# The gate as four wide products, and moved halves and stores, in a one-core diffusion layer

## The reference

```python
def adaln(cond, w_ada, b_ada):
    mod = jax.nn.silu(cond) @ w_ada + b_ada
    shift, scale, gate = jnp.split(mod[:, None, :], 3, axis=-1)
...
        h_l = rmsnorm(x_l, norm_g[l]) * (1.0 + sc) + sh
        u_l = h_l @ w_in[l]
...
        out_l = mixer(u_l, keys_all, lp, rope, True)
...
        x_l = x_l + gt * (out_l @ w_out[l])
    return rmsnorm(x_l, final_norm_g)
```

## Time and profile before

| | us |
|---|---|
| median of 3 runs | 985.48 |
| lowest and highest | 983.87, 987.82 |
| the profiled execution, its own time | 985.1 |
| its span, first to last instruction | 983.3 |
| PE busy | 951.1 (97%) |
| DVE busy | 619.1 (63%) |
| ACT busy | 398.9 (41%) |
| POOL busy | 95.6 (10%) |

### The profile page before, as it was taken

How to read it: one execution, slowest core, us unless ns; L and a number is a source line. 1 busy time by engine, 2 the same in 40 slices (tenths; PEclk the granted TensorE clock), 3 DMA queues, 4 the chain that set the end, 5 groups by cost and what they waited for, 6 DMA issues and landing times.

```text
span 983.3 us, 12611 instructions
## 1 busy us (share of the span) xinstructions
PE 951.1 (97%) x5074; PEld 788.2 (80%) x5074; DVE 619.1 (63%) x821; ACT 398.9 (41%) x626; POOL 95.6 (10%) x77
## 2 busy tenths in 40 slices
PE   5999999989999999999999999999999999999996
PEld 3777787778888889888888888888888888888885
DVE  2776989777756676746785563767777765513154
ACT  3555665544234433322323432645445452212224
POOL 1222200300002200000003360000000000202020
PEclk8999999999999999999999999999999999999999
DMA  9999922222232221258784233101002117222224
GB/s 366 426 423 395 339 87 84 86 65 65 86 95 86 72 80 43 86 171 292 257 300 149 86 87 127 43 12 43 12 1 86 44 57 286 86 86 86 95 77 171
DMA packets 28838, 136.17 MB, mean 138 GB/s; under 512 B 3595, under 2 KB 4043, under 8 KB 21740
## 3 DMA queue, kind: packets, MB, share of 16 engines
q1 hardware_dynamic: 28060, 134.71, 38.2%
q10 hardware_dynamic: 720, 0.66, 0.2%
HBM read 131.16 MB, written 4.19 MB: 138 GB/s over the span
## 4 chain that ended last, share of the span: by engine, by line
PE 77%; DVE 11%; DMA 5%; ACT 4%; issue 2%; SPq 0%; ACTq 0%; DVEq 0%
PE pp L1717 28%; PE pp L2023 18%; PE pp L1747 17%; PE pp L1664 4%; PE pp L1641 2%; DMA w_raw<-in_wb_dram 2%; PE pp L1986 2%; DMA wa_raw<-in_wa_dram 2%; DMA ada_raw<-in_w_ada_dram 1%; PE pp L1668 1%; DVE w_lo L1139 1%; DVE gate_acc L1150 1%; DVE pt_lo L1409 1%; ACT w_hi L616 1%; PE pp L1978 1%
## 5 line engine op out<-in xcount | busy, mean ns | idle before, releaser
L1717 PE MATMUL pp<-h_hi,w_hi 128*128 128x512 f32 x544 | 215.9, 397 | 2.1 <-DVE w_lo L1139 1.2
L1717 PE MATMUL pp<-h_lo,w_hi 128*128 128x512 f32 x544 | 213.1, 392 | 0.0
L1717 PE MATMUL pp<-h_hi,w_lo 128*128 128x512 f32 x544 | 212.8, 391 | 0.0
L1139 DVE TENSOR_TENSOR w_lo<-w_raw,w_hi 128x1024 fp32r<-128x1024 f32 x68 | 87.2, 1282 | 100.7 <-ACT w_hi L616 100.4
L616 ACT ACTIVATE w_hi<-w_raw 128x1024 fp32r<-128x1024 f32 x68 | 72.0, 1058 | 176.7 <-PE pp L1717 129.4
L1717 PEld LDWEIGHTS pp<-h_hi,w_hi 128*128 128x128 f32 x544 | 102.9, 189 | 27.1 <-DVE w_lo L1139 4.2
L1717 PEld LDWEIGHTS pp<-h_hi,w_lo 128*128 128x128 f32 x544 | 102.8, 189 | 21.9
L1717 PEld LDWEIGHTS pp<-h_lo,w_hi 128*128 128x128 f32 x544 | 103.0, 189 | 21.4 <-issue 0.8
L2023 PE MATMUL pp<-wo_hi,m_hi 128*128 128x512 f32 x256 | 100.6, 393 | 0.0
L2023 PE MATMUL pp<-wo_hi,m_lo 128*128 128x512 f32 x256 | 99.6, 389 | 0.0
L2023 PE MATMUL pp<-wo_lo,m_hi 128*128 128x512 f32 x256 | 99.6, 389 | 0.0
(11 more groups left out here) (309 smaller groups left out, 1874.8 us busy)
## 6 DMA issues: line engine op xcount, KB each, us to landing
w_raw<-in_wb_dram SPq DMA_DIRECT2D x68, 512.0 KB, 3.6
ada_raw<-in_w_ada_dram SPq DMA_DIRECT2D x15, 2048.0 KB, 12.2
w_gate_raw<-in_w_gate_dram SPq DMA_DIRECT2D x16, 1024.0 KB, 4.9
wo_raw<-in_w_out_dram SPq DMA_DIRECT2D x16, 1024.0 KB, 4.7
wa_raw<-in_wa_dram SPq DMA_DIRECT2D x16, 320.0 KB, 7.0
UG<-in_xT_dram SPq DMA_DIRECT2D x8, 512.0 KB, 8.4
y<-in_x_dram SPq DMA_DIRECT2D x4, 1024.0 KB, 9.2
wh_raw<-in_w_heads_dram SPq DMA_DIRECT2D x4, 768.0 KB, 4.7
```

What stands on the lines that cost most here:

```text
L1139: eng.tensor_tensor(lane(wb_lo, n % KW), lane(wb_raw, n % KW), lane(wb_hi, n % 2), ALU.subtract).then_inc(wb_lo_done, 1)
L1717: mm = eng.matmul(ps[i][:], w, x, start=(kk == 0 and m == 0), stop=(kk == KT - 1 and m == 2))
```

## The change

- **Gate sums**: `gate_sums` now makes 4 products, with the 128x128 tile of ones as the weights and 512 columns of `gate_acc` as the moving side. Each gives the sums in all 128 rows alike, in banks 2, 3, 6 and 7. At n = 65 DVE's `gate_rows_done` adds them to `gate_rows`, where SP has put the bias row 128 times by a DMA of its own; SP issues it at its n = 65, behind the load of chunk 65, and first waits for `pool_done`. `gate_rows` lies in tiles 25 to 28 now. PE waits for `gate_out` before the first head. `gcol`, its bias columns in `par`, and the diagonals with their products and copy are gone.
- **Places of `w_out`**: the second and third place of `wo_raw` move; their first loads wait for the last values (`v_mm`) and the last scores (`s_mm`, 32).
- **Root**: on ACT at n = 9 the three `context_shift` come behind root, `turned` and `biased`.
- **Key halves**: on DVE at i = 6 `keys(2 * p + 2, 1)` comes ahead of `gate` and `rope_low`.
- **Last tile**: of the last token tile ACT scales block 0 alone and stores it, then stores block 3; POOL scales block 1; SP stores blocks 2 and 1.

```diff
-        wo_places = (FREE, 25, FREE + 5)
+        wo_places = (FREE, FREE + 5, FREE + 10)
...
+                if slot == 63:
+                    eng.wait_ge(pool_done, 4)
+                    eng.dma_start(gate_rows_[:], t["b_gate"].to_broadcast([P, D])).then_inc(gate_in[0], 16)
...
             load_out(0)
-            eng.wait_ge(pool_done, 4)
+            eng.wait_ge(v_mm, 12)
             load_out(1)
-            eng.wait_ge(v_mm, 12)
+            eng.wait_ge(s_mm, 32)
             load_out(2)
...
+            eng.wait_ge(gained, 12)
+            eng.wait_ge(row_scale, 4)
+            yy = y_out[:, 3 * D + L:3 * D + 2 * L]
+            eng.tensor_scalar(yy, yy, rs[:, 11:12], None, ALU.mult).then_inc(gained, 1)
...
-                for q in range(2):
+                for q in range(1 if tok == 3 else 2):
...
-                    if tok == 3:
-                        eng.wait_ge(fin_act, 7 + q)
-                        eng.dma_start(out[3 * P:4 * P, q * L:(q + 1) * L], yy).then_inc(stored, 16)
+            eng.wait_ge(fin_act, 7)
+            eng.dma_start(out[3 * P:4 * P, 0:L], y_out[:, 3 * D:3 * D + L]).then_inc(stored, 16)
+            eng.wait_ge(fin_done, 8)
+            eng.dma_start(out[3 * P:4 * P, 1536:D], y_out[:, 3 * D + 1536:4 * D]).then_inc(stored, 16)
...
-            def gate_columns():
+            def gate_rows_done():
                 eng.wait_ge(comb_mm, KT + 1)
-                eng.tensor_tensor(gcol[:], ps[7][:, 0:16], par[:, P_BG:P_BG + 16], ALU.add)
+                eng.wait_ge(gate_in[0], 16 * 8 + 16)
+                for i, b in enumerate((2, 6)):
+                    x = gate_rows_[:, i * 1024:(i + 1) * 1024].rearrange("p (a b) -> p a b", a=2)
+                    ins = eng.tensor_tensor(x, psum[:, b:b + 2, :], x, ALU.add)
+                ins.then_inc(gate_out, 1)
...
-            for i in range(16):
-                if i >= 4:
-                    eng.wait_ge(gate_mm, i - 3)
-                eng.tensor_scalar(out_tmp[:, (i % 4) * P:(i % 4 + 1) * P], ident[:], gcol[:, i:i + 1], None, ALU.mult).then_inc(diag_done, 1)
-            eng.wait_ge(gate_mm, 16)
-            eng.tensor_copy(gate_rows_[:].rearrange("p (a b) -> p a b", a=4), psum[:, 4:8, :]).then_inc(gate_out, 1)
...
-                for c in range(16):
-                    mm = eng.matmul(ps[7][:, c:c + 1], gate_acc[:, c * P:(c + 1) * P], ones[:, 0:1], start=True, stop=True)
+                for c, b in enumerate((2, 3, 6, 7)):
+                    mm = eng.matmul(ps[b][:], ones[:], gate_acc[:, c * L:(c + 1) * L], start=True, stop=True)
...
-            for i in range(16):
-                eng.wait_ge(diag_done, i + 1)
-                eng.matmul(psum[:, 4 + i // 4, (i % 4) * P:(i % 4 + 1) * P], ones[:], out_tmp[:, (i % 4) * P:(i % 4 + 1) * P],
-                           start=True, stop=True).then_inc(gate_mm, 1)
```

More of the change, by code:

```diff
@@ L31 @@
 HF = L // 2
-P_BSH, P_BSC, P_BG, P_NG = 0, 16, 32, 48
-P_CW, P_CB, P_HB, P_QG, P_KG, P_PS = 64, 100, 112, 120, 124, 126
-N_PAR = 130
+P_BSH, P_BSC, P_NG = 0, 16, 32
+P_CW, P_CB, P_HB, P_QG, P_KG, P_PS = 48, 84, 96, 104, 108, 110
+N_PAR = 114
 T_POOL, T_Q = 13, 17
@@ L142, in backbone @@
         wo_high_ = [at("wo_hi0", 19, 2048, F32R), at("wo_hi1", FREE + 16, 2048, F32R)]
-        gate_rows_, gain, y_out = at("gate_rows", FREE + 10, D), at("gain", TAB + 10, D), at("y", FREE + 21, 4 * D)
+        gate_rows_, gain, y_out = at("gate_rows", 25, D), at("gain", TAB + 10, D), at("y", FREE + 21, 4 * D)
         out_tmp, ss, rs = at("out_tmp", TAB + 14, L), at("row_sums", TAB + 15, 16), at("row_scale", TAB + 15.25, 12)
@@ L287, in backbone @@
         wo_in = [sem(f"wo_in{s}") for s in range(3)]
-        mix_hi, mix_lo, diag_done, gate_mm, gate_out = sem("mix_hi"), sem("mix_lo"), sem("diag_done"), sem("gate_rows_mm"), sem("gate_out")
+        mix_hi, mix_lo, gate_out = sem("mix_hi"), sem("mix_lo"), sem("gate_out")
         wo_hi, wo_lo, wo_mm, mm_done = sem("wo_hi_done"), sem("wo_lo_done"), sem("wo_mm"), sem("wo_bank_mm")
@@ L444, in _ @@
             for i in range(4):
[L445 to L448, removed]
+                eng.wait_ge(fin_done, 2 * i + (1 if i == 3 else 2))
+                a, b = 1024, 1536 if i == 3 else D
+                eng.dma_start(out[i * P:(i + 1) * P, a:b], y_out[:, i * D + a:i * D + b]).then_inc(stored, 16)
                 if i < 3:
                     eng.wait_ge(fin_act, 2 * i + 2)
-                    eng.dma_start(out[i * P:(i + 1) * P, 0:1024], y_out[:, i * D:i * D + 1024]).then_inc(stored, 16)
+                    a, b = 0, 1024
+                else:
+                    eng.wait_ge(gained, 13)
+                    a, b = L, 2 * L
+                eng.dma_start(out[i * P:(i + 1) * P, a:b], y_out[:, i * D + a:i * D + b]).then_inc(stored, 16)
             eng.wait_ge(stored, 160)
@@ L895, in _ @@
                         context(i)
-                if n == 9:
-                    for i in range(3):
-                        context_shift(i)
                 if n == 12:
@@ L947, in _ @@
                             product_high(m)
+                if n == 9:
+                    for i in range(3):
+                        context_shift(i)
                 if n % 4 == 3 and n not in (TF[0] + 3, TF[1] + 3):
@@ L1556, in _ @@
                 if i == 6:
+                    if p < 3:
+                        keys(2 * p + 2, 1)
                     gate(2 * p)
@@ L1590, in _ @@
                     rope_low(2 * p + 2)
-                    keys(2 * p + 2, 1)
                 if i == 7:
@@ L1905, in _ @@
             eng.wait_ge(kr_cut, 4)
+            eng.wait_ge(gate_out, 1)
             def queries(h):
@@ L2117, in alloc @@
             return ctx.enter_context(nc.sbuf_tensor(name, [P, cols], F32))
-        mem = {n: alloc(n, c) for n, c in (("par", N_PAR), ("gcol", 16), ("ident", P), ("ones", P), ("eps", 1))}
+        mem = {n: alloc(n, c) for n, c in (("par", N_PAR), ("ident", P), ("ones", P), ("eps", 1))}
         base = (nc.sbuf_base + 31) // 32 * 32
@@ L2201, in layout @@
         "w_heads": np.ascontiguousarray(w_heads),
-        "x": np.ascontiguousarray(f["x"][0]), "gain": f["final_norm_g"].reshape(1, D),
+        "x": np.ascontiguousarray(f["x"][0]), "gain": f["final_norm_g"].reshape(1, D), "b_gate": b_ada[2 * D:].reshape(1, D),
         "w_out": np.ascontiguousarray(f["w_out"][0].reshape(4, 4, P, 4, L).transpose(3, 0, 2, 1, 4)).reshape(16, P, 4 * L),
```

11 lines of the change are left out of this document (4 added, 7 removed).

## The result

The changed kernel takes **973.73 us** (median of 4 runs, 973.39 to 974.10); the kernel before, run on the same chip beside it, takes 985.10 (983.87 to 987.82). The ratio is 0.9886, with a 95% interval of 0.9874 to 0.9899. The forecast was 973.5. The profiled execution of the changed kernel took 973.39, with a span of 971.6 us against 983.3.

The account below looks back on a forecast made before the run. TensorE, busy 97% of 983.3 us, was taken as the bound. Gains 4.64 + 0.0 + 1.78 + 3.57 + 1.89 + 0 = 11.88 gave a forecast median of 973.5 us (971.5 to 975.5; wider range 971.5 to 978.5).

Parts of the forecast that it names:

- Root: Step 9 on ACT: earlier root removes 3.05 us of PE's wait and 1.59 of slow-clock products; gain 4.64 us.
- Rival A: Slow clock behind the root gap and gate sums does not come back; 1.59 + 1.78 lost, 976.9 us; chance 0.10.
- Gate sums: Four wide products cost the same as 16 one-column ones, but the clock stays up behind them; gain 1.78 us, bounds 0 to 1.9.
- Gate rows: Output stage: 16 diagonal products between two chunks disappear from PE, DVE's replacement additions are hidden; gain 3.57 us.
- The bias row: Its 1 MB DMA on SP ahead of chunk 66's load takes some 4.9 us and delays nothing PE needs; cost 0.
- can push it by about 1.3: Delay in us that the bias row's load could cause to chunk 66's load behind it, to 588.4.
- Rival C: Slower: bias row lands late and DVE stands still in step 65; 31 us after issue would give 990.8; chance 0.03.
- Keys: Heads, sixth step of a pair: k_lo moved in front removes three PE waits of 0.63; gain 1.89 us, bounds 0 to 2.1.
- Rival B: Waits are replaced: PE, earlier, meets the next wait (pt_lo, or ACT's moved activations); 975.4 to 978.4 us; chance 0.12.
- Places and waits of `w_out`: Later loads are wanted only after the last head; 0 taken, up to 4.9 us for a late load.
- Last tile: Tail: sooner issue looks like 0.7 us, but the 16 DMA engines bound it; 0 taken, bounds -0.5 to +0.7.
- rival D: The tail gives its 0.7 us after all; 972.8 us; chance 0.05.

Follow-up runs that it names:

- experiment 1: Changed kernel with the six shift-column additions ahead of the root on ScalarE again; 976.94 us, ratio 0.9915.
- experiment 2: Kernel of experiment 1 plus 13 unused 128x512 products on TensorE where it would wait for the root; 976.32 us.
- experiment 3: Changed kernel with its four gate-sum products replaced by the earlier 16 one-column products (128x1); 976.94 us, ratio 0.9915.
- experiment 9: Changed kernel without GpSimd's last scaling, that quarter of the last tile stored without its row scale; 973.59 us.
- experiment 10: Changed kernel with its whole tail undone: ScalarE scales both quarters of the last tile, nothing on GpSimd; 974.52 us, ratio 0.9903.
- experiment 7: Changed kernel with the bias row loaded a second time ahead of the load of chunk 66; 973.69 us.
- experiment 11: Changed kernel with VectorE's low half of the first w_out chunk moved from step 26 to step 29 of the heads; 973.27 us.

## Why the prediction was right, and where it was not

**Root, 4.64 forecast, 4.63 and 4.60 measured.** Both halves are right (3.02 and 1.57 in experiment 1), and experiment 2 parts them. Rival A fell in the profiled executions; two faster runs of experiment 1 leave it open there. The moved activations delayed nothing: no wait stands at chunk 11. The Trainium skill (TensorE: Matmul & The Clock Gate, What's actually happening) also says that the number of slow products differs from run to run of one kernel. No kernel here was traced twice, so no run shows just that; what the traces have is the same one-column products in two kernels, with an excess of 1.75 us in the kernel before and 3.40 in experiment 3.

**Gate sums, 1.78 forecast, 1.74 measured; upper bound too low.** The four products took 3.43, inside the forecast. My bound of 1.9 for the clock's part was taken from one execution. Experiment 3 lost 3.40.

**Gate rows, 3.57 forecast, 3.59 measured.** VectorE's additions were hidden as said: they started at 587.56 without idle time, 2.35 us for both.

**The bias row, cost 0 as forecast, cover mis-sized.** The step that failed is "can push it by about 1.3": the load landed 7.6 us after issue and not 3.6, a push of 4.0. Instead of over 3 us of cover there were 0.8. The working counted the bytes ahead of the load at full rate and nothing else. But 1.52 of the 1.57 MB had moved only at 582.7, 5.0 us after the load's issue, where in the kernel before all bytes of this load had moved about 3.1 us after its issue. That is about half of the push; the other half is the stretch in which almost nothing moved, and its cause is open. Rival C stays unlikely from the other side: the row itself landed in 4.7 us, close to the 4.9 assumed.

**Keys, 1.89 forecast, 2.54 measured (2.44 undone); over my upper bound of 2.1.** The mechanism was right. The step that failed is "3 x 0.63 = 1.89": the term was mis-sized because I took the idle time of the row for the cost of the wait, where start to start gives 0.87. Rival B fell: `pt_lo` kept its 1.4 and 1.4.

**Places and waits of `w_out`, 0 forecast.** The 720 products of the output stage run as one piece, so PE waited for none of these loads.

**Last tile, 0 forecast, -0.10 measured; right for one of its two reasons only.** DMA bound it, as experiments 9 and 10 show, and rival D fell. But the sooner issue that I granted never came: first to last issue is 1.44 us (967.01 to 968.45) against 1.39 in the earlier trace rows. My "POOL's scaling takes 0.62 to 0.95" failed. Timeline of VectorE and GpSimd in the changed kernel, then VectorE in experiment 9:

```profile
966.90 1.18 DVE L1644 SCALAR_TENSOR_TENSOR y<-y,row_scale,gain 128x512 f32<-128x512 f32 x1
...
966.64 1.78 POOL L524 TENSOR_SCALAR y<-y,row_scale 128x512 f32<-128x512 f32 x1 [34.64 <-DVE row_scale L1639]
```

```profile
966.91 0.75 DVE L1641 SCALAR_TENSOR_TENSOR y<-y,row_scale,gain 128x512 f32<-128x512 f32 x1
```

GpSimd's scaling takes 1.78 us, and VectorE's instruction beside it 1.18 where it takes 0.75 alone. The Trainium skill (SBUF — State Buffer, SBUF: two separate sides) says that the two engines share a pair of ports by an exclusive lock, and that an instruction of VectorE with two inputs from the memory contends for it with GpSimd. The trace agrees that GpSimd's work delays VectorE's, by 0.43. GpSimd's scaling started first and was longer too, by over 0.8 against the earlier trace rows, where the rule by itself lets the first one run undisturbed; no run here has that scaling without VectorE beside it, so its cause is open.

**Not in the sum:** the opening (-1.17, cause open) and 0.43 us between 222 and 492 us. In the kernel before, the chain in that piece runs from 449 to 488 us through three loads of `w_raw` behind the gate's weights (6.26, 8.08 and 5.96 us); in the changed kernel it stays on PE. Of the 14 traces three have their chain there (the kernel before, experiments 7 and 11), with waits of PE on `w_lo` of 0.49 and 1.00 us in the last two, and the others no such wait. The changed kernel and its variants do the same work there, and take 269.3 to 270.1 us for this piece where it can be cut; the 269.73 of before lie in that range, so the 0.43 need not be the change's. I did not test what decides it.

## What to carry to other kernels

Price a wait from the start of the instruction ahead to the start of the one behind, in both orders, and not by the idle time of the row. Compare the pieces that the change should leave alone too: here they moved by 1.17 and 0.43 us. Where PE idles for 3 us or passes single columns, look at the granted clock behind it, and count the slow products as part of what the gap costs, with a wide bound. Before work is spread over a third engine, see whether the end is bound by the transfers, and how long that engine and its neighbour take side by side.

## What was not expected

- One-column products let the granted clock fall to 0.50 with PE busy all the time, for 1.75 us of loss in one execution and 3.40 in another; products of 128 columns with the ones as weights, as many and about as long, did not.
- A load of 0.5 MB behind a row of 1 MB read 128 times took 7.6 us to land (3.5 without it), with the DMA engines nearly idle for 1.4 of the last 2.6 us; a second such row added only 0.9 us.
- A 128x512 scaling on GpSimd took 1.78 us beside VectorE (0.62 to 0.95 elsewhere), and VectorE's instruction beside it 1.18 in place of 0.75.
